# A state-space scan: the swap of real and imaginary halves moves from TensorE to VectorE

## The reference

```python
bu_re = einsum('bsgc,gpc->bsgp', ug, bbar_re); bu_im = ...
_, _, xr, xi = associative_scan(combine, (ar_t, ai_t, bu_re, bu_im), axis=1)
y = einsum('gcp,bsgp->bsgc', c_re, xr) - einsum('gcp,bsgp->bsgc', c_im, xi)
```

## Time and profile before

| what | value |
|---|---|
| median of 3 runs | 1265.19 us (1260.91 to 1266.45) |
| span of the profiled execution, first to last instruction | 1255.9 us |
| own time of the profiled execution | not given beside the three runs |
| the median less the span | 9.3 us |
| PE busy | 1225.1 us, 98% of the span |
| DVE busy | 879.0 us, 70% |
| ACT busy | 507.2 us, 40% |
| POOL busy | 485.8 us, 39% |

### The profile page before, as it was taken

One profiled execution on the slowest core, in us unless ns is written; L12 is line 12 of the kernel. 1 busy time (PEld: TensorE's weight loads), 2 busy tenths in 40 slices (PEclk: granted clock), 3 DMA queues, 4 the chain that ended last, 5 costly groups with the idle time before them and its releaser, 6 DMA issues.

```text
span 1255.9 us, 16148 instructions
## 1 busy us (share of the span) xinstructions
PE 1225.1 (98%) x6074; PEld 990.3 (79%) x6074; DVE 879.0 (70%) x1415; ACT 507.2 (40%) x840; POOL 485.8 (39%) x336
## 2 busy tenths in 40 slices
PE   7999999999999999999979999999999999999998
PEld 4787788887788788888848777888777788888886
DVE  5787777867387776986577487778655887677252
ACT  4454224753443343333243632266443344333331
POOL 0143433243463235555405333423435443245551
PEclk9999999999999999999979999999999999999999
DMA  9532211132322435464434212212323322465322
GB/s 360 199 134 68 60 59 54 64 116 70 102 66 77 130 86 204 165 234 141 162 100 166 86 52 64 71 34 74 129 67 92 102 60 86 116 232 194 98 83 67
DMA packets 63437, 142.01 MB, mean 113 GB/s; under 512 B 29440, under 2 KB 31616, under 8 KB 62592
## 3 DMA queue, kind: packets, MB, share of 16 engines
q1 hardware_dynamic: 54016, 137.84, 32.9%
q10 hardware_dynamic: 9344, 3.15, 1.0%
HBM read 128.12 MB, written 10.49 MB: 110 GB/s over the span
## 4 chain that ended last, share of the span: by engine, by line
PE 94%; DMA 1%; DVE 1%; SPq 1%; ACT 1%; issue 1%; POOL 0%; ACTq 0%; DVEq 0%
PE bank L1672 25%; PE bank L1674 24%; PE bank L1673 24%; PE bank L1852 4%; PE bank L1808 2%; PE bank L1818 1%; PE bank L1832 1%; PE bank L1906 1%; DMA arena<-in_wada 1%; PE bank L1921 1%; PE bank L1939 1%; PE bank L1940 1%; PE bank L1825 1%; PE bank L1926 1%; PE bank L1896 1%
## 5 line engine op out<-in xcount | busy, mean ns | idle before, releaser
L726 POOL TENSOR_TENSOR w_lo<-raw,w_hi 128x512 fp32r<-128x512 f32 (+1 forms) x166 | 236.8, 1426 | 748.6 <-ACT w_hi L760 748.5
L1672 PE MATMUL bank<-h_hi,w_hi 128*128 128x512 f32 x896 | 361.7, 404 | 3.8 <-ACT arena L837 1.6
L1674 PE MATMUL bank<-h_hi,w_lo 128*128 128x512 f32 x896 | 349.3, 390 | 0.0
L1673 PE MATMUL bank<-h_lo,w_hi 128*128 128x512 f32 x896 | 348.9, 389 | 0.0
L760 ACT ACTIVATE w_hi<-raw 128x1024 fp32r<-128x1024 f32 (+2 forms) x170 | 178.8, 1055 | 226.9 <-PE bank L1674 199.7
L727 POOL TENSOR_TENSOR w_lo<-raw,w_hi 128x512 fp32r<-128x512 f32 (+2 forms) x166 | 256.4, 1545 | 0.0
L1672 PEld LDWEIGHTS bank<-h_hi,w_hi 128*128 128x128 f32 x896 | 168.3, 188 | 48.2 <-issue 12.3
L1673 PEld LDWEIGHTS bank<-h_lo,w_hi 128*128 128x128 f32 x896 | 168.4, 188 | 38.5 <-issue 5.0
L1674 PEld LDWEIGHTS bank<-h_hi,w_lo 128*128 128x128 f32 x896 | 168.2, 188 | 35.7
L1672 PE MATMUL bank<-w_hi,h_hi 128*128 128x512 f32 (+1 forms) x256 | 97.8, 382 | 5.4 <-issue 3.6
L1673 PE MATMUL bank<-w_lo,h_hi 128*128 128x512 f32 (+1 forms) x256 | 95.7, 374 | 0.0
(11 more groups left out here) (282 smaller groups left out, 1830.2 us busy)
## 6 DMA issues: line engine op xcount, KB each, us to landing
raw<-in_wfull SPq DMA_DIRECT2D x170, 512.0 KB, 3.6
arena<-in_wada SPq DMA_DIRECT2D x48, 512.0 KB, 4.7
x_scratch<-xm SPq DMA_DIRECT2D x2, 2048.0 KB, 8.8
arena<-x_scratch SPq DMA_DIRECT2D x2, 2048.0 KB, 9.1
arena<-in_x SPq DMA_DIRECT2D x4, 512.0 KB, 6.6
arena<-in_s5m SPq DMA_DIRECT2D x2, 1024.0 KB, 5.6
u_scratch<-arena ACTq DMA_DIRECT2D x4, 512.0 KB, 4.5
arena<-u_scratch SPq DMA_DIRECT2D x8, 256.0 KB, 3.8
```

The source lines that it names most:

```text
L726: nc.gpsimd.tensor_tensor(lo[:, :half], raw_chunk(n)[:, :half], hi[:, :half].bitcast(F32), ALU.subtract)
L1672: mm(out_, a_hi, b_hi, start=first, stop=False)
L1673: mm(out_, a_hi, b_lo, start=False, stop=False)
L1674: return mm(out_, a_lo, b_hi, start=False, stop=last)
```

## The change

Both swaps by matmul go. In their place DVE writes the sine product in two instructions of 64 partitions each, each reading one half and writing the other. The subtraction and the scan's last addition read `v2` from SBUF instead of a PSUM bank. The parts 5 and 3 of each quarter become one part 3, at the place in the list where part 5 was (directly behind part 2 for quarters 0 and 2). The ring of banks hands out two fewer per quarter. PE's part 4 and DVE's reuse of the buffers now wait for the semaphore `z_ready`.

```diff
@@ schedule: the plan's lines, cut to the steps that change
-        steps += cm("ag", 1, 0) + s5(0, 2, 5) + load("mtin", 0, 0) + tab(1, 1, 2, 3) + gate("ag", 0, 1) + cm("ag", 1, 1)
-        steps += cm("mg1", 0, 0) + gate("ag", 1, 0, 1) + s5(0, 3) + cm("mg1", 0, 1) + load("mtin", 0, 1) + load("uin", 1) + load("mtin", 1, 0)
+        steps += cm("ag", 1, 0) + s5(0, 2, 3) + load("mtin", 0, 0) + tab(1, 1, 2, 3) + gate("ag", 0, 1) + cm("ag", 1, 1)
+        steps += cm("mg1", 0, 0) + gate("ag", 1, 0, 1) + cm("mg1", 0, 1) + load("mtin", 0, 1) + load("uin", 1) + load("mtin", 1, 0)
         steps += s5(1, 1) + load("mtin", 1, 1) + load("ysave", 0) + tab(2, 0) + s5(0, 4) + load("yback", 0) + s5(1, 2) + tab(2, 1)
-        steps += cm("wb1", 0) + s5(1, 5) + cm("mg1", 1, 0) + s5(2, 1) + s5(1, 3) + tab(2, 2) + load("mtin", 2, 0) + tab(2, 3)
-        steps += load("mtin", 2, 1) + tab(3, 0) + cm("mg1", 1, 1) + s5(1, 4) + load("uin", 2) + load("uin", 3) + s5(2, 2, 5) + tab(3, 1)
-        steps += load("ysave", 1) + cm("wb1", 1) + gelu(0, 0) + cm("mg1", 2, 0) + s5(2, 3) + s5(3, 1) + load("ysave", 2) + tab(3, 2, 3)
-        steps += load("yback", 1) + s5(2, 4) + s5(3, 2) + load("mtin", 3, 0) + gelu(0, 1) + cm("mg1", 2, 1) + s5(3, 5) + load("mtin", 3, 1)
-        steps += gelu(1, 0) + gelu(2, 0) + cm("wb1", 2) + s5(3, 3) + cm("mg1", 3, 0) + load("yback", 2) + gelu(1, 1) + load("ysave", 3)
+        steps += cm("wb1", 0) + s5(1, 3) + cm("mg1", 1, 0) + s5(2, 1) + tab(2, 2) + load("mtin", 2, 0) + tab(2, 3)
+        steps += load("mtin", 2, 1) + tab(3, 0) + cm("mg1", 1, 1) + s5(1, 4) + load("uin", 2) + load("uin", 3) + s5(2, 2, 3) + tab(3, 1)
+        steps += load("ysave", 1) + cm("wb1", 1) + gelu(0, 0) + cm("mg1", 2, 0) + s5(3, 1) + load("ysave", 2) + tab(3, 2, 3)
+        steps += load("yback", 1) + s5(2, 4) + s5(3, 2) + load("mtin", 3, 0) + gelu(0, 1) + cm("mg1", 2, 1) + s5(3, 3) + load("mtin", 3, 1)
+        steps += gelu(1, 0) + gelu(2, 0) + cm("wb1", 2) + cm("mg1", 3, 0) + load("yback", 2) + gelu(1, 1) + load("ysave", 3)
@@ ring of banks
-    "s5": lambda s: ((), (0, 1, 2, 3), (4,), (6,), (7,), (5,))[s[3]],
+    "s5": lambda s: ((), (0, 1, 2, 3), (4,), (), (7,))[s[3]],
@@ DVE
+            def turn_halves(to, x_, by):
+
+                mark(v.tensor_tensor(to[0:SP_], x_[SP_:], by[SP_:], ALU.mult))
+                return mark(v.tensor_tensor(to[SP_:], x_[0:SP_], by[0:SP_], ALU.mult))
+
             def s5_states(l, j, key):
...
                 if j:
-                    wait_read(dve, (("s5", l, j - 1), 6))
+                    dve.wait_ge(z_ready, q_no)
                     wait_full(dve, (("s5", l, j - 1), 7))
...
-                v.tensor_tensor(v2, b1, tsin, ALU.mult).then_inc(w_ready, 1)
+                swapped = turn_halves(v2, b1, tsin)
                 v.tensor_tensor(zz, b1, tcos, ALU.mult).then_inc(read((key, 4)), 1)
-                return turn
...
+                after(swapped)
+                wait_read(dve, (key, 4))
+                then_wait(v.tensor_tensor(zz, zz, v2, ALU.subtract))
+
+            def s5_scan(l, j):
...
-                v.tensor_tensor(zz, zz, src, ALU.subtract).then_inc(read((key, 5)), 1)
                 if q_no:
                     dve.wait_ge(y_saved, 16 * q_no)
...
                 then_wait(v.tensor_tensor_scan(flat[0], flat[1], flat[2], 0.0, ALU.mult, ALU.add))
-                v.tensor_tensor(v2, tt, tsin, ALU.mult).then_inc(v_ready, 1)
                 mark(v.tensor_tensor(zz, tt, tcos, ALU.mult))
...
+                after(turn_halves(v2, tt, tsin))
+                v.tensor_tensor(zz, zz, v2, ALU.add).then_inc(z_ready, 1)
@@ PE
-                    if part == 5:
-                        pe.wait_ge(w_ready, q_no + 1)
-                        dst = wait_free(pe, (key, 5))
-                        mm(dst[:], swap, v2.rearrange("p g n -> p (g n)"), start=True, stop=True
-                           ).then_inc(full((key, 5)), 1)
-                    if part == 3:
-                        pe.wait_ge(v_ready, q_no + 1)
-                        dst = wait_free(pe, (key, 6))
-                        mm(dst[:], swap,
-                           v2.rearrange("p g n -> p (g n)"), start=True, stop=True).then_inc(full((key, 6)), 1)
                     if part == 4:
                         pe.wait_ge(mt_in, 16 * CH * (q_no + 1))
-                        wait_read(pe, (key, 6))
+                        pe.wait_ge(z_ready, q_no + 1)
```

More of the change, by code:

```diff
@@ L491, in program @@
         bank = [ctx.enter_context(nc.psum_tensor(f"bank{n}", [P, S], F32)) for n in range(8)]
-        ident, swap, ones = cst[:, 0:128], cst[:, 64:192], cst[:, 192:320]
+        ident, ones = cst[:, 0:128], cst[:, 192:320]
         invf, nidx = cst[:, 320:384], cst[:, 384:448]
@@ L534, in program @@
             sem("s5_ang"), sem("s5_trig"), sem("s5_w"), sem("s5_tab_ang"), sem("s5_tab"))
-        kt_ready, mt_in, mt_clear, v_ready = sem("kt_ready"), sem("mt_in"), sem("mt_clear"), sem("v_ready")
-        w_ready = sem("w_ready")
+        mt_in, mt_clear, z_ready = sem("mt_in"), sem("mt_clear"), sem("z_ready")
         y_saved, ycm_in = sem("y_saved"), [sem(f"ycm{j}_in") for j in range(NW)]
@@ L1189, in s5_tables @@
                     if j >= 2:
-                        wait_read(dve, (("s5", l, j - 2), 6))
+                        dve.wait_ge(z_ready, q_no - 1)
                     ang, near = tsin2[j % 2], tcos2[j % 2]
@@ L1202, in s5_states @@
                 if j:
-                    wait_read(dve, (("s5", l, j - 1), 6))
+                    dve.wait_ge(z_ready, q_no)
                     wait_full(dve, (("s5", l, j - 1), 7))
-                turn = mark(v.tensor_copy(m8[:, :, 1:], s5s[:, 5, gs].unsqueeze(2).broadcast_to([P, QG, NCH - 1])))
+                mark(v.tensor_copy(m8[:, :, 1:], s5s[:, 5, gs].unsqueeze(2).broadcast_to([P, QG, NCH - 1])))
                 dve.wait_ge(s5_tab, q_no + 1)
                 b1 = wait_full(dve, (key, 4))[:].rearrange("p (g n) -> p g n", g=QG)
-                v.tensor_tensor(v2, b1, tsin, ALU.mult).then_inc(w_ready, 1)
+                swapped = turn_halves(v2, b1, tsin)
                 v.tensor_tensor(zz, b1, tcos, ALU.mult).then_inc(read((key, 4)), 1)
-                return turn
-            def s5_scan(l, j, key, turn):
+                after(swapped)
+                wait_read(dve, (key, 4))
+                then_wait(v.tensor_tensor(zz, zz, v2, ALU.subtract))
+            def s5_scan(l, j):
                 q_no = NW * l + j
                 tsin, tcos = tsin2[j % 2], tcos2[j % 2]
-                src = wait_full(dve, (key, 5))[:].rearrange("p (g n) -> p g n", g=QG)
-                wait_read(dve, (key, 4))
-                v.tensor_tensor(zz, zz, src, ALU.subtract).then_inc(read((key, 5)), 1)
                 if q_no:
                     dve.wait_ge(y_saved, 16 * q_no)
-                after(turn)
-                wait_read(dve, (key, 5))
                 flat = [a.rearrange("p g n -> p (g n)") for a in (tt, m8, zz)]
                 then_wait(v.tensor_tensor_scan(flat[0], flat[1], flat[2], 0.0, ALU.mult, ALU.add))
-                v.tensor_tensor(v2, tt, tsin, ALU.mult).then_inc(v_ready, 1)
                 mark(v.tensor_tensor(zz, tt, tcos, ALU.mult))
[L1227 to L1231, removed]
+                after(turn_halves(v2, tt, tsin))
+                v.tensor_tensor(zz, zz, v2, ALU.add).then_inc(z_ready, 1)
             replaced, sum_done = {}, [0, 0]
@@ L1599, in _ @@
                     if part == 2:
-                        turned = s5_states(l, j, step[:3])
-                    if part == 5:
-                        s5_scan(l, j, step[:3], turned)
+                        s5_states(l, j, step[:3])
                     if part == 3:
-                        s5_turned(l, j, step[:3])
+                        s5_scan(l, j)
                 if kind == "gelu":
```

## The result

The changed kernel takes 1279.81 us (median of four runs, 1275.03 to 1286.11), the kernel before, on the same chip, 1265.49 us (1260.91 to 1266.45): a ratio of 1.0127 [1.0092, 1.0162]. It is slower by 14 us, where 2.7 us less were forecast, and it lies above the forecast's 1250 to 1267. The profiled execution of the changed kernel is the slowest of its four (1286.11 us, span 1284.3), that of before was a quick one (span 1255.9), so the two traces differ by more than the medians do.

The account below looks back on a forecast made before the run. PE, 98% busy, was taken as the bound, though nearly held by other engines at three places per layer. Net per layer 0.7 - 1.72 - 0.36 = -1.3 us; two layers -2.7, so 1265.2 - 2.7 = 1262.5 us, range 1250 to 1267.

Parts of the forecast that it names:

- A: Quarter 0's part 4: PE arrives 2.7 us earlier but waits for ACT's L972, 0.5 us later; quarter 0's whole gain lost.
- B: Quarter 2's part 2: PE, ahead by only 0.36 us, waits under 1 us for the load of u.
- C: Quarter 2's part 4: PE idles some 3 to 4 us for ACT's L972 and is 0.7 us late.
- e: DVE's extra time for each quarter, forecast at 1.5 us, with bounds 0.3 and 5.5.
- the slack of 0.99: Quarter 0: ACT's wait for PE at L920 before the change, the only slack on ACT's way to L972, 0.99 us.
- the swaps' gain: On PE: 16 swaps by 0.86 us, 13.8 us; with the removed waits 18.3 us if nothing else holds PE.
- R1: Rival: PE is the only bound, so the whole 18.3 us is won, 1246.9 us; chance 0.20.
- At nothing: Items priced at zero, among them later DVE table work for quarters 1 and 3, where PE arrives 3 us after them.
- R3: Rival: DVE instructions reading only SBUF contend with POOL and cost 0.9 us more each, 1277 us; chance 0.10.
- DVE's busy time: Sign of a right forecast: DVE busy about 18 us more, since every added instruction is counted whole.
- The distance between span and time: The kernel before: median time 9.3 us above the profiled span of 1255.9 us, kept for the changed kernel.
- R2: Rival: half products on DVE are cheap, 0.35 us each, giving 1258.5 us; chance 0.10.

Follow-up runs that it names:

- e1_fill: The changed kernel plus four unread matmuls on constants ahead of part 4 of quarters 0 and 2: 1263.55 us, ratio 1.0005 to the kernel before.
- e7_fill0: The changed kernel plus four unread matmuls ahead of part 4 of quarter 0 only: 1269.46 us, ratio 1.0053 to the kernel before.
- e8_gelu: The changed kernel without fills, with gelu(0, 0) moved behind quarter 3's first part: 1265.51 us, ratio 1.0019 to the kernel before.
- e10_dve_fill: e4_more_dve plus five unread matmuls per layer where its trace had PE idle: 1265.44 us, ratio 1.0028 to the kernel before.
- e2_whole: The changed kernel with whole products in place of half products, the exchange of halves left out: 1273.19 us, ratio 1.0066 to the kernel before.
- e4_more_dve: The kernel before, swaps kept, with the cosine product behind the scan computed three times instead of once: 1276.64 us, ratio 1.0108.

## Why the prediction was wrong

**Place by place the waits at A, B and C were about right.** Place A: "PE arrives 2.7 us earlier" and 0.5 late gave 3.2; the traces have 3.45 in both layers, ended by ACT's L971. The timeline of ACT shows the chain. Its wait for DVE's tables is 14.23 - 12.42 = 1.8 us longer than in the earlier trace rows, which is e; from there to L971 it takes 403.45 - 395.08 = 8.4 us where it took 399.74 - 390.37 = 9.4, since the slack of 0.99 at L919 is used up:

```profile
395.08 0.63 ACT L961 ACTIVATE arena<-arena 128x512 f32<-128x512 f32 x1 [14.23 <-DVE arena L1195]
...
401.53 1.08 ACT L919 ACTIVATE sig<-bank 128x512 f32<-128x512 f32 x2
...
403.45 1.05 ACT L971 ACTIVATE arena<-bank 16x512 f32<-16x512 f32 x2
```

Place B: under 1 us for the load of u; measured 0.97 and 0.42. Place C: 3 to 4 us; measured 2.16 and 2.94, somewhat less, behind ACT's wait for the GELU step:

```profile
458.42 0.63 ACT L988 ACTIVATE arena<-arena 128x512 f32<-128x512 f32 x1 [7.12 <-DVE arena L1605]
```

That the swaps' gain would mostly be lost in these waits is therefore right, and so is R1's rejection. Whether the forecast's net -2.7 us would have come at full clock no run shows: e1_fill, with the clock kept at places A and C but four matmuls more at each, lies at +0.1 us, and the two spans less their clock loss differ by -5.9 us, an estimate.

**The step that failed: a wait of PE was priced at its own length.** "PE arrives 2.7 us earlier ... and waits: quarter 0's whole gain is lost, and 0.5 more" counts the idle time and nothing behind it. Behind the waits at A and C the clock was at 1.2 GHz for some 14 to 17 us each, which is 6.8 to 8.5 us by the windows, and behind the wait at B of layer 0 for 7 us, which is 3.4; that it is a real price e1_fill, e7_fill0, e8_gelu and, on the kernel before, e10_dve_fill show by taking it away. It is a term that the working did not have at all. The trace of before had it, in the windows from 640 to 660 us around the waits of 2.25, 3.00 and 3.58 us; the prediction reads the granted clock nowhere. The Trainium skill, TensorE: Matmul & The Clock Gate, section HAM oscillation, describes a kernel whose waits for data send the clock down again and again; this trace agrees (0.50 behind the wait of 3.45 us). A rival on the slower side ought to have stood in the prediction with A and C as its places. At up to 6.8 us for each of the four waits there, the price of the one dip in the trace of before, it would have given up to 27 us more than the forecast, and 17 came.

**The size of e.** Forecast 1.5, measured 1.8 (6.99 against 5.20). A half costs a whole product, as taken from the copy of 64 partitions. The 0.3 are the held starts: in three places of the sum the next instruction starts 0.72 us on and not 0.61, which is 0.33; subtraction and scan take 0.09 less than assumed, the awaited ends 0.05 more. The prediction had quoted the Trainium skill, VectorE: DVE Perf Modes, section Two Vector instructions with no wait between them, for just 0.3, and went by the rows; the measurement sides with the page, whose rule it had worked out to e = 1.8. It is small: 1.2 us in the sum, as was said there.

**"At nothing: ... the later DVE work for tables of quarters 1 and 3, where PE arrives 3 us after them."** Wrong in layer 1: PE waits 2.39 us at the first part of quarter 3 for DVE's L1164, after a wait of 3.45 at A, and before one of 2.94 at C:

```profile
1083.99 1.92 PE L1900 MATMUL bank<-arena 128*16 128x128 f32 x16 [2.39 <-DVE arena L1164]
```

Nearly all of this wait is a stretching of the table work that the change didn't touch. Two of its instructions took 2.45 and 2.44 us beside POOL's split, where they take 1.35 in the earlier trace rows and in layer 0 of the same trace (rows of the changed kernel):

```profile
1077.40 1.56 POOL L725 TENSOR_TENSOR w_lo<-raw,w_hi 128x512 fp32r<-128x512 f32 x1 [5.79 <-ACT w_hi L759]
1077.73 2.45 DVE L1162 TENSOR_TENSOR arena<-pw,arena 128x1152 f32<-128x1152 f32 x1
...
1080.10 2.44 DVE L1163 TENSOR_TENSOR arena<-pw,arena 128x1152 f32<-128x1152 f32 x1
```

The wait of 3.23 us in e1_fill has the same cause (2.44 and 2.43 us). So a DVE that is 1.8 us late can meet POOL where it did not meet it before; this is R3's mechanism at a place where R3 had no price. In e8_gelu PE waits at the same line in layer 0 as well, 1.3 us, once C no longer holds it. The prediction compared the tables with PE's arrival in the trace of before, not with the arrival of a PE that runs ahead.

**DVE's busy time.** "About 18 us more", measured 9.2. The sentence counts too many instructions: four half products take the place of two whole ones, so two are added per quarter, 16 in all (1431 against 1415), and 16 x 0.61 = 9.8. The time that matters, from the first product to the table work, grew by 1.8 us in quarters 0 and 2, for the starts and the awaited ends are in it and in no busy time.

**The distance between span and time.** The prediction kept 9.3 us between them. In the changed kernel's executions time and span lie 1.8 us apart, in those of the other kernels 1.7 to 2.9; the rest is that the profiled execution of before was a quick one. It moves nothing in the difference.

**The rivals.** R1 (1246.9) is excluded by the waits. R2 is excluded by the 0.69 and 0.72 us. R3, the only one that ended slower, gave 1277 us, close to the 1279.8 measured, but by luck: contention lengthens some instructions (the eight L1227 of the changed kernel take 937 ns in the mean, L1216 693), but e1_fill has such long ones as well (its half products that read SBUF alone take 933 and 808 ns in the mean) and loses nothing against before. Where contention costs PE time, it is in the tables of layer 1, 2.4 us.

**Open.** Which waits let the clock fall isn't settled: it stayed behind 3.23 us at 449 us of e1_fill and fell at 1.00 us at 1051 us of the same execution. Nor is it known whether the split of the loss between A and C is the same in every execution; the four runs of the changed kernel, 11 us apart, suggest that it is not.

## What to carry to other kernels

Before you take work off an engine that is 98% busy, ask at each of its meetings with the others what it will wait for next; where that engine is TensorE, read the granted clock behind the waits that the trace already has, and price a new wait with what it cost there, not with its length. If a wait can't be removed, move the late step or give PE something harmless to do: sixteen unread matmuls, four at each of four waits, were worth some 15 us here, and nine 3 us in the kernel before. And judge a change of this kind together with its reordering: alone it lost 1.3%, with two small edits it came out 0.3% ahead of the kernel before, with the list rewritten and fills 0.6%, of which fills without the change give 0.2%.

## What was not expected of the hardware

Taking 14 us of matmuls out of the busiest engine, with no instruction added anywhere, made the kernel slower by 0.66% (e2_whole), and putting matmuls back whose results nobody reads made it faster. Waits of as little as 1.00 us (e1_fill) and 1.44 us (e4_more_dve) stood at the start of stretches of some 7 us at half the granted clock. And a product over 64 partitions that reads one half and writes the other lasts 0.69 us, as one over the whole 128 partitions does, and starts stand 0.72 us apart in place of 0.61.
